# Layer norms between the stages of a two-block model: order of shifts and copies, splits per pair of tiles, place of the sums, and the queue of two small loads

## The chip, the cores and the metric

The kernel runs on one core of a Trainium2 chip, in one launch. The metric is the time of the execution on the device in microseconds (us), lower is better. A run gives one time; the median of several is compared. The profile is of one further execution.

## What is computed

Two transformer-like blocks over x of 512 tokens by 1024 channels, all in float32. The part that matters here is what stands between the matrix products: after each residual addition there is a norm over the 1024 channels of a token, and its result is the input of the next product.

```python
def first_block(...):
    h = x + mixer(rmsnorm(x, g_mix))              # conv, pooling, then y @ w_out   ("out")
    h = h + swiglu(rmsnorm(h, g_ffn), ...)        # norm 1; gate/up "gu0", "down0"
    return rmsnorm(h, g_final)                    # norm 2

def second_block(x, ...):                         # alpha = DN_ALPHA = sqrt(2)
    h = fox_attention(x)                          # "qkv1", "out1"
    x = layer_norm(alpha * x + h, g, b)           # norm 3
    x = layer_norm(alpha * x + conv_ffn(x), g, b) # "gu1", "down1", norm 4
    k1, k2, v = shared_kv(x)                      # rotary tables cos, sin
    h = diff_attention(x, k1, k2, v)              # "qkv2", "out2"; uses lambda
    x = layer_norm(alpha * x + h, g, b)           # norm 5
    x = layer_norm(alpha * x + conv_ffn(x), g, b) # "gu2", "down2", norm 6
    return x

def layer_norm(x, g, b):
    mu = mean(x); var = mean((x - mu) ** 2)
    return (x - mu) * rsqrt(var + 1e-5) * g + b
```

## The kernel before

Channels lie on the 128 partitions, in DT = 8 tiles of 128; tokens are the free axis, S = 512 wide. The residual is `xres` (128 x 8 x 512). For precision every product is done as three: an operand X is split into a high part XH (rounded to the fast matmul format) and a low part XL = X - XH, and likewise each weight tile into WH and WL; `product` (L875 to L877) multiplies XL with WH, XH with WH and XH with WL.

**Weights** come in items of up to 128 x 8 x 128. SyncE loads an item into one of two buffers `raw` (L482; it waits for `w_lo`, the split of the item two before). ScalarE writes WH in two instructions (`high`, L1371), GpSimd writes WL in two (`low`, L675), into one of four slots; TensorE then uses the item. A slot comes free with `item_done`.

**A norm in halves.** The six norms m = 1 to 6 at the ends of the stages out, down0, out1, down1, out2 and down2 are done for two halves h of 256 tokens, so that the first half can be normed while TensorE still works on the second half of the last items. Norms 1 and 2 are RMS norms; norms 3 to 6 are centred (mean and shift). The order of work is written out by hand on each engine:

- TensorE, end of the old stage (`stage`, `down`): the first half of the last two items (`half_item` or `part` with h = 0), the second half of the item before the last (24 products of 128x256), `half_stats(m, 0)` (one-column products that sum x and x squared over the channels, L1044 and L1046; 24 of them in norms 3 and 5), the first 6 of 8 steps of the last item's second half, `half_widen(m, 0)` (root and mean are spread over the partitions, L1033), the last 2 steps. Then the new stage begins in `stage_in_halves`: for each half and tile k four products with XH (L971, L972; wait for `x_top`) and, one tile behind, two with XL (L959; wait for `x_lo`). `half_stats(m, 1)` stands at tile 2 and `half_widen(m, 1)` at tile 4 of the first half.
- VectorE (`norm_in_halves`, L1845 to L1869): adds the tail tiles, computes the moments from the sums, and norms tiles in pairs. For norms 3 to 6 a pair is one multiplication by the root (L1865, both tiles, 128x512, one operand in PSUM) and one multiply-and-add for each tile (L1869, 128x256, its inputs `xres` and the shift buffer in SBUF). For norms 1 and 2 it is one instruction for each tile (L1861), with an operand in PSUM. Each signals `xn_ready`. The order is pair 0, second half's tail, pairs 1 and 2, the moments of the second half, pair 3, then the four pairs of the second half.
- ScalarE (`norm_in_halves`, L1397 to L1421): squares of the tail (L1397), the root (L1381), and `pair(h, p)`: `shifts` (L1408, one 128x256 instruction for each tile, into one of three pair buffers, free again when VectorE has used it), then a copy of each tile into XH (L1421, 128x256, signals `x_top`). The next pair's shifts stand behind the copies of this one. Between the halves it does `high` of the new stage's third item.
- GpSimd (`lows_of_halves`): for each tile XL = x - XH (L708, 128x256, signals `x_lo`), with `low` of the third item between the halves.

**Two small loads** are issued by ScalarE in the middle of a norm, through the argument `tail_done`: `load_gates` in norm 2 (2 DMAs) and `load_rope` in norm 4 (6 DMAs: the rotary tables, 128x512 in one and four of 32x512, and the lambda parameters). Both first wait for the last item of the old stage, since their buffers overlap with those of the stage. VectorE waits for the rope tables after norm 4; ScalarE waits for the gates after norm 2. SyncE at that time has issued the first four weight items of the new stage; its fifth (loop index n = 4) waits for the split of the third.

## Time and profile before

| what | value |
|---|---|
| median of 3 runs | 1907.21 us (1903.19 to 1908.96) |
| profiled execution | 1903.91 us, of which the span from first to last instruction 1902.1 us |
| TensorE busy | 1829.4 us (96%) |
| GpSimd busy | 1036.0 us (54%) |
| ScalarE busy | 781.4 us (41%) |
| VectorE busy | 768.8 us (40%) |
| mean granted TensorE clock | 0.979 |

Engines are written PE (TensorE), DVE (VectorE), ACT (ScalarE), POOL (GpSimd) and SP (SyncE); a q behind a name marks the engine's queue of DMA issues. A row of the timeline gives the start in us from the begin of the span, the time that the instruction (or the group "xN" of equal neighbours) took, the line of the kernel, output and inputs, their shape, and in brackets the idle time before it with what ended it. "issue" means that the profile shows nothing that was waited for.

### The profile page before, as it was taken

The numbers are of one execution on the slowest core, as the hardware profiler recorded it, in microseconds if no ns is written. First come the engines' busy times: TensorE is split into PE (matmuls) and PEld (weight loads), VectorE is DVE, ScalarE is ACT, GpSimd is POOL, SyncE is SP. The second block draws the span as 40 slices with busy tenths as digits, with TensorE's granted clock in tenths as the row PEclk, the third lists the DMA queues.
The fourth block names the chain that finished last, engine by engine and source line by source line (L and its number), as shares of the span: only waits on it lengthen the run. The fifth ranks groups of instructions, "written<-read, shape, count | busy, mean of one in ns | idle before, by whom it ended". The sixth has DMA issues, their size and how long they took to land.

```text
span 1902.1 us, 27192 instructions
## 1 busy us (share of the span) xinstructions
PE 1829.4 (96%) x8895; PEld 1522.8 (80%) x8895; DVE 768.8 (40%) x1389; ACT 781.4 (41%) x1638; POOL 1036.0 (54%) x937
## 2 busy tenths in 40 slices
PE   6999999999999999899999999889998999999997
PEld 5878888888887888788888888878886888888887
DVE  6964000001135455564333322456655743333224
ACT  4433332322244455345444422445554454444223
POOL 5866655655462322356666654555554566666551
PEclk7999999999999999999999999899999999999998
DMA  4303333323333444223333233233232233332331
GB/s 123 100 18 94 100 92 103 91 84 105 90 99 95 118 112 115 75 76 93 95 99 99 77 106 93 68 78 84 69 80 67 73 94 97 90 99 86 99 91 67
DMA packets 328499, 170.88 MB, mean 90 GB/s; under 512 B 43426, under 2 KB 318964, under 8 KB 328436
## 3 DMA queue, kind: packets, MB, share of 16 engines
q1 hardware_dynamic: 327026, 169.49, 32.1%
q10 hardware_dynamic: 1410, 0.59, 0.1%
q8 instruction: 35, 0.57, 0.1%
q14 instruction: 28, 0.23, 0.0%
HBM read 151.10 MB, written 2.10 MB: 81 GB/s over the span
## 4 chain that ended last, share of the span: by engine, by line
PE 79%; ACT 4%; DVE 4%; SPq 3%; issue 3%; DMA 3%; POOL 3%; ACTq 0%; DVEq 0%; POOLq 0%
PE bank L875 23%; PE bank L877 22%; PE bank L876 22%; PE attended L875 2%; PE attended L876 2%; PE attended L877 2%; SPq L639 2%; DMA raw<-in_kv_w 1%; DVE xres L1869 1%; DVE small L2027 1%; POOL XL L708 1%; ACT pmap L1582 1%; POOL WL L675 1%; ACT XH L1421 1%; PE turned L1212 1%
## 5 line engine op out<-in xcount | busy, mean ns | idle before, releaser
L675 POOL TENSOR_TENSOR WL<-raw,WH 128x512 fp32r<-128x512 f32 (+3 forms) x656 | 786.0, 1221 | 618.5 <-ACT WH L1371 617.7
L875 PE MATMUL bank<-XL,WH 128*128 128x512 f32 x1456 | 580.5, 399 | 10.0 <-ACT work L1597 5.2
L877 PE MATMUL bank<-XH,WL 128*128 128x512 f32 x1456 | 568.8, 391 | 0.0
L876 PE MATMUL bank<-XH,WH 128*128 128x512 f32 x1456 | 567.7, 390 | 0.0
L1371 ACT ACTIVATE WH<-raw 128x512 fp32r<-128x512 f32 (+3 forms) x656 | 338.4, 566 | 352.1 <-PE bank L877 197.1
L875 PEld LDWEIGHTS bank<-XL,WH 128*128 128x128 f32 x1456 | 275.0, 189 | 65.5 <-issue 8.1
L877 PEld LDWEIGHTS bank<-XH,WL 128*128 128x128 f32 x1456 | 274.7, 189 | 58.1
L876 PEld LDWEIGHTS bank<-XH,WH 128*128 128x128 f32 x1456 | 275.4, 189 | 51.6
L877 PE MATMUL bank<-HH,WL 128*128 128x512 f32 (+1 forms) x528 | 201.1, 381 | 0.0
L876 PE MATMUL bank<-HH,WH 128*128 128x512 f32 (+1 forms) x528 | 201.1, 381 | 0.0
L875 PE MATMUL bank<-HL,WH 128*128 128x512 f32 (+1 forms) x528 | 201.0, 381 | 0.0
L1978 DVE SCALAR_TENSOR_TENSOR xres<-xres,bank 128x512 f32 (+1 forms) x39 | 26.7, 686 | 267.2 <-PE bank L877 266.8
L790 POOL TENSOR_TENSOR HL<-hid,HH 128x512 f32 x66 | 85.1, 1289 | 70.5 <-ACT HH L1537 70.5
L876 PEld LDWEIGHTS bank<-HH,WH 128*128 128x128 f32 x528 | 99.1, 188 | 21.2
L877 PEld LDWEIGHTS bank<-HH,WL 128*128 128x128 f32 x528 | 99.1, 188 | 21.2
L875 PEld LDWEIGHTS bank<-HL,WH 128*128 128x128 f32 x528 | 99.1, 188 | 21.1
L1582 ACT ACTIVATE pmap<-score,small 128x128 f32<-128x128 f32 (+3 forms) x128 | 67.1, 525 | 90.6 <-DVE small L2027 90.5
L2001 DVE TENSOR_TENSOR hid<-bank,act_g 128x512 f32<-128x512 f32 x21 | 14.5, 692 | 207.4 <-PE bank L877 203.9
L2027 DVE TENSOR_REDUCE small<-score 128x1 f32<-128x128 f32 (+3 forms) x128 | 62.4, 488 | 80.7 <-PE score L1197 52.0
L2084 DVE SCALAR_TENSOR_TENSOR hid<-bank,par,hid 128x511 f32<-128x511 f32 x42 | 31.5, 750 | 150.7 <-ACT hid L1660 150.5
L1660 ACT ACTIVATE hid<-bank,par 128x512 f32<-128x512 f32 x42 | 32.7, 779 | 143.5 <-PE bank L877 143.5
L2084 DVE SCALAR_TENSOR_TENSOR act_g<-bank,par,act_g 128x511 f32<-128x511 f32 x42 | 31.5, 750 | 128.2 <-ACT act_g L1660 128.2
(278 smaller groups left out, 2579.3 us busy)
## 6 DMA issues: line engine op xcount, KB each, us to landing
raw<-in_ffn_w_in SPq DMA_DIRECT2D x88, 512.0 KB, 3.8
raw<-in_w_gate SPq DMA_DIRECT2D x22, 512.0 KB, 3.8
raw<-in_w_up SPq DMA_DIRECT2D x22, 512.0 KB, 3.9
raw<-in_ffn_w_out SPq DMA_DIRECT2D x28, 384.0 KB, 3.4
raw<-in_ffn_w_out SPq DMA_DIRECT2D x28, 320.0 KB, 3.1
raw<-in_a_w_in SPq DMA_DIRECT2D x16, 512.0 KB, 4.1
raw<-in_kv_w SPq DMA_DIRECT2D x32, 256.0 KB, 3.8
raw<-in_w_in SPq DMA_DIRECT2D x12, 512.0 KB, 3.9
```

What stands on the lines that cost most here:

```text
L639: sp.dma_start(z[r, c, :].bitcast(F32), x[r, slot, 0, :].bitcast(F32)).then_inc(q_padded, 16)
L675: pool.tensor_tensor(wl, x, wh, ALU.subtract).then_inc(w_lo, 1)
L790: pool.tensor_tensor(HL[:, bass.ds(it * 2 + j, 1), :], hid[:, j:j + 1, :], HH[:, bass.ds(it * 2 + j, 1), :].bitcast(F32), ALU.subtract).th ...
L875: pe.matmul(out_, wh, xl, start=start, stop=False)
L876: pe.matmul(out_, wh, xh, start=False, stop=False)
L877: return pe.matmul(out_, wl, xh, start=False, stop=stop)
L1371: act.activation(wh, x, ACT.Copy).then_inc(w_hi, 1)
L1582: act.activation(pmap[:, n % 4, 0:k], sc[c][:, 0:k], ACT.Exp, bias=small[:, n % 4:n % 4 + 1], accum_out=small[:, 4 + n % 4:5 + n % 4]).the ...
L1660: act.activation(dst[:, j, :], ff_banks(it, j)[side][:, :], ACT.Identity, bias=ff_par(layer - 1, 3, n), scale=ff_par(layer - 1, 2, n)).the ...
L1978: dve.scalar_tensor_tensor(out=r, in0=r, scalar=factor, in1=bank[j][:, :].rearrange("p (a s) -> p a s", a=1), op0=ALU.mult, op1=ALU.add).t ...
L2027: dve.tensor_reduce(small[:, n % 4:n % 4 + 1], sc[c][:, 0:(n // 2 + 1) * P], AX_X, ALU.max, negate=True).then_inc(mx[c], 1)
L2084: own.link(dve.scalar_tensor_tensor(out=dst[:, j, 1:], in0=src[:, 0:S - 1], scalar=ff_par(layer - 1, 1, n), in1=dst[:, j, 1:], op0=ALU.mul ...
```

## The change

Five edits:

1. On ScalarE `pair` is taken apart into `shifted_pair` (shifts) and `tops` (copies). The shifts of pair p+1 stand ahead of the copies of pair p; in the second half `copies(0)` (output copies, norm 6 only) moves behind the shifts of pair 2.
2. Copies into XH and the splits XL = x - XH are done for two tiles by one instruction (128x512), except for tiles 0 and 1 of each half (`TILES_OF_HALF`).
3. On TensorE `half_stats(m, 0)` stands behind the first 4 of 8 steps of the half item, instead of behind all 8, in `stage` and in `down`.
4. `load_gates` is issued by SyncE at n = 4 of the qkv1 loop, ahead of the weight load of that index.
5. `load_rope` is issued by SyncE at n = 4 of the qkv2 loop, likewise.

```diff
+TILES_OF_HALF = ((0, 1), (1, 1), (2, 2), (4, 2), (6, 2))
...
+            def load_gates():
+                sp.wait_ge(item_done, STAGES["qkv1"][0])
+                sp.dma_start(wf[:, :, :], a_in[:, :, 3 * D:3 * D + FOX_HEADS]).then_inc(wf_in, 16)
+                sp.dma_start(small[0:FOX_HEADS, 48:49], A["a_b_f_2"].rearrange("o h -> h o")).then_inc(wf_in, 16)
...
             for n in range(4 * UNITS + 8):
                 u, j = divmod(n - 4, 4)
+                if n == 4:
+                    load_gates()
...
+            def load_rope():
+                sp.wait_ge(item_done, STAGES["qkv2"][0])
+                sp.dma_start(rope[:, 0, :], A["rope"][0]).then_inc(rope_in, 16)
+                for b in range(4):
+                    r = 0 if b >= 2 else 32
+                    sp.dma_start(rope[32 * b:32 * b + 32, 1, :], A["rope"][1][r:r + 32, :]).then_inc(rope_in, 16)
+                sp.dma_start(lamr[:, :], A["b_lambda_2"].rearrange("o a d -> o (a d)")).then_inc(rope_in, 16)
...
                 u, j = divmod(n - 5, 4)
+                if n == 4:
+                    load_rope()
...
-                    for t in range(DT):
-                        i = DT * h + t
-                        pool.wait_ge(x_top, half_tile(m, h, t) + 1)
-                        src = pairs_of[i // 2 % 3][:, i % 2, :] if m == 1 else xres[:, t, c]
-                        pool.tensor_tensor(XL[:, t, c], src, XH[:, t, c].bitcast(F32), ALU.subtract).then_inc(x_lo, 1)
+                    for t, n in TILES_OF_HALF:
+                        src = pairs_of[(DT * h + t) // 2 % 3][:, t % 2:t % 2 + n, :] if m == 1 else xres[:, t:t + n, c]
+                        pool.wait_ge(x_top, half_tile(m, h, t) + n)
+                        pool.tensor_tensor(XL[:, t:t + n, c], src, XH[:, t:t + n, c].bitcast(F32), ALU.subtract).then_inc(x_lo, n)
...
-                half_item(name, DT - 2, 0, hi, lo, 0, DT, 1).then_inc(item_done, 1)
+                half_item(name, DT - 2, 0, hi, lo, 0, DT, 1, 0, 4)
                 half_stats(m, 0)
+                half_item(name, DT - 2, 0, hi, lo, 0, DT, 1, 4).then_inc(item_done, 1)
...
-                part(2, 1).then_inc(item_done, 1)
+                part(2, 1, 0, 4)
                 half_stats(m, 0)
+                part(2, 1, 4).then_inc(item_done, 1)
...
-                def pair(h, p):
+                def tops(h, p):
+                    if not follower:
+                        return
                     c = slice(h * HALF, (h + 1) * HALF)
+                    for t, w in TILES_OF_HALF:
+                        if t // 2 != p:
+                            continue
+                        act.wait_ge(xn_ready, DT + half_tile(m, h, t) + w)
+                        src = pairs_of[(DT * h + t) // 2 % 3][:, t % 2:t % 2 + w, :] if m == 1 else xres[:, t:t + w, c]
+                        act.activation(XH[:, t:t + w, c], src, ACT.Copy).then_inc(x_top, w)
+
+                def shifted_pair(h, p):
                     if n in CENTRED:
                         shifts(h, p)
-                    if not follower:
-                        return
-                    for t in (2 * p, 2 * p + 1):
-                        i = DT * h + t
-                        act.wait_ge(xn_ready, DT + half_tile(m, h, t) + 1)
-                        src = pairs_of[i // 2 % 3][:, i % 2, :] if m == 1 else xres[:, t, c]
-                        act.activation(XH[:, t, c], src, ACT.Copy).then_inc(x_top, 1)
 
                 squares_of(0)
                 root(n, 0)
-                pair(0, 0)
+                shifted_pair(0, 0)
+                shifted_pair(0, 1)
+                tops(0, 0)
                 squares_of(1)
                 tail_done()
-                pair(0, 1)
-                pair(0, 2)
+                shifted_pair(0, 2)
+                tops(0, 1)
+                shifted_pair(0, 3)
+                tops(0, 2)
                 root(n, 1)
-                pair(0, 3)
+                tops(0, 3)
                 if follower:
                     high(Nth(STAGES[follower][0] + 2), UNIT[2] if follower[0] == "q" else DT)
-                for p in range(DT // 2):
-                    pair(1, p)
-                    if p == 1:
-                        copies(0)
+                shifted_pair(1, 0)
+                shifted_pair(1, 1)
+                tops(1, 0)
+                shifted_pair(1, 2)
+                copies(0)
+                tops(1, 1)
+                shifted_pair(1, 3)
+                tops(1, 2)
+                tops(1, 3)
                 copies(1)
...
-            norm_in_halves(2, "qkv1", tail_done=load_gates)
+            norm_in_halves(2, "qkv1")
...
-            norm_in_halves(4, "qkv2", "ffn", load_rope)
+            norm_in_halves(4, "qkv2", "ffn")
```

## Rows read from the trace of the kernel before

**Rows 1.** The page, part 1: busy us, share and instructions of each engine.
```profile
PE 1829.4 (96%) x8895; PEld 1522.8 (80%) x8895; DVE 768.8 (40%) x1389; ACT 781.4 (41%) x1638; POOL 1036.0 (54%) x937
```

**Rows 2.** Windows, norm 3: stretch, busy us of PE, PEld, DVE, ACT, POOL, clock.
```profile
835.80:858.90 23.10, 17.93 (x126) 16.69 (x126) 16.55 (x33) 16.70 (x39) 14.26 (x18) 0.93 0.08 24
```

**Rows 3.** Timeline of TensorE in norm 3; columns as told above.
```profile
836.80 0.38 PE L971 MATMUL bank<-XH,WH 128*128 128x256 f32 x1 [1.00 <-ACT XH L1421]
...
839.40 0.39 PE L971 MATMUL bank<-XH,WH 128*128 128x256 f32 x1 [1.15 <-ACT XH L1421]
...
840.22 0.28 PE L1044 MATMUL turned<-ones,work 128*128 128x1 f32 x2
...
842.82 0.36 PE L971 MATMUL bank<-XH,WH 128*128 128x256 f32 x1
...
858.81 0.40 PE L875 MATMUL attended<-XL,WH 128*128 128x512 f32 x1
```

**Rows 4.** Timeline of ScalarE in norm 3, second half: copies, shifts, copies.
```profile
854.24 0.81 ACT L1421 ACTIVATE XH<-xres 128x256 fp32r<-128x256 f32 x2 [0.51 <-DVE xres L1869]
854.96 1.00 ACT L1408 ACTIVATE work<-turned,par 128x256 f32<-128x256 f32 x2
856.49 0.82 ACT L1421 ACTIVATE XH<-xres 128x256 fp32r<-128x256 f32 x2 [0.52 <-DVE xres L1869]
```

**Rows 5.** Timelines of VectorE and GpSimd in norm 3, single instructions.
```profile
848.91 1.49 DVE L1869 SCALAR_TENSOR_TENSOR xres<-xres,par,work 128x256 f32<-128x256 f32 x1
848.66 1.47 POOL L675 TENSOR_TENSOR WL<-raw,WH 128x512 fp32r<-128x512 f32 x1
...
853.37 0.83 DVE L1869 SCALAR_TENSOR_TENSOR xres<-xres,par,work 128x256 f32<-128x256 f32 x1 [0.41 <-ACT work L1408]
853.19 0.74 POOL L708 TENSOR_TENSOR XL<-xres,XH 128x256 fp32r<-128x256 f32 x1
```

**Rows 6.** Single lines over the span: duration ns min/median/max, shapes.
```profile
L790 POOL TENSOR_TENSOR HL<-hid,HH x66: 1276/1289/1301, 193.9 to 1761.2; 128x512 f32 x66
L1371 ACT ACTIVATE WH<-raw x656: 293/617/636, 12.4 to 1865.0; 128x512 fp32r<-128x512 f32 x109, 128x384 fp32r<-128x384 f32 x36, 128x256 fp32r<-128x256 f32 x19
```

**Rows 7.** Timelines in norm 4: ScalarE with its queue, TensorE, SyncE's queue.
```profile
1214.50 0.36 ACTq L1680 DMA_DIRECT2D rope<-in_rope  x1
...
1217.37 1.02 ACT L1408 ACTIVATE work<-score,par 128x256 f32<-128x256 f32 x2 [2.48 <-issue]
...
1219.03 0.58 PE L971 MATMUL bank<-XH,WH 128*128 128x256 f32 x1 [3.43 <-ACT XH L1421]
...
1229.96 0.37 SPq L616 DMA_DIRECT2D raw<-in_b_w_q  x1
```

**Rows 8.** Windows: the stretches at half clock, and the one ahead of norm 4's.
```profile
844.20:847.60 3.40, 3.40 (x19) 3.40 (x17) 2.24 (x5) 2.96 (x7) 1.58 (x3) 0.50 0.00 0
...
1212.90:1216.30 3.40, 1.70 (x13) 1.29 (x11) 1.86 (x5) 1.81 (x5) 1.44 (x2) 1.00 0.13 35
1216.30:1229.90 13.60, 10.87 (x51) 10.87 (x52) 7.31 (x17) 7.42 (x18) 5.79 (x8) 0.50 0.10 31
```

**Rows 9.** Timelines in norm 1 (GpSimd, TensorE) and norm 2 (TensorE).
```profile
184.16 5.61 POOL L708 TENSOR_TENSOR XL<-work,XH 128x256 fp32r<-128x256 f32 x8
...
190.16 0.40 PE L875 MATMUL attended<-XL,WH 128*128 128x512 f32 x1
...
545.70 0.39 PE L971 MATMUL bank<-XH,WH 128*128 128x256 f32 x1 [0.46 <-ACT XH L1421]
```

**Rows 10.** Timeline of VectorE in norm 6.
```profile
1884.54 0.88 DVE L1869 SCALAR_TENSOR_TENSOR xres<-xres,par,work 128x256 f32<-128x256 f32 x2 [0.47 <-ACT work L1408]
...
1893.69 0.90 DVE L1869 SCALAR_TENSOR_TENSOR xres<-xres,par,work 128x256 f32<-128x256 f32 x2 [0.32 <-ACT work L1408]
```

**Rows 11.** Timelines in norm 2: ScalarE's square of the tail, TensorE's first sum.
```profile
537.29 0.40 ACT L1397 ACTIVATE work<-xres 128x256 f32<-128x256 f32 x1
...
539.26 0.28 PE L1044 MATMUL score<-ones,work 128*128 128x1 f32 x2
```

More of the change, by code:

```diff
@@ L1557, in _ @@
             warm(ACT.Sqrt)
-            def load_gates():
-                act.wait_ge(item_done, STAGES["qkv1"][0])
-                act.dma_start(wf[:, :, :], a_in[:, :, 3 * D:3 * D + FOX_HEADS]).then_inc(wf_in, 16)
-                act.dma_start(small[0:FOX_HEADS, 48:49], A["a_b_f_2"].rearrange("o h -> h o")).then_inc(wf_in, 16)
-            norm_in_halves(2, "qkv1", tail_done=load_gates)
+            norm_in_halves(2, "qkv1")
             act.wait_ge(wf_in, 32)
@@ L1676, in _ @@
             warm(ACT.Sqrt)
-            def load_rope():
-                act.wait_ge(item_done, STAGES["qkv2"][0])
-                act.dma_start(rope[:, 0, :], A["rope"][0]).then_inc(rope_in, 16)
-                for b in range(4):
-                    r = 0 if b >= 2 else 32
-                    act.dma_start(rope[32 * b:32 * b + 32, 1, :], A["rope"][1][r:r + 32, :]).then_inc(rope_in, 16)
-                act.dma_start(lamr[:, :], A["b_lambda_2"].rearrange("o a d -> o (a d)")).then_inc(rope_in, 16)
-            norm_in_halves(4, "qkv2", "ffn", load_rope)
+            norm_in_halves(4, "qkv2", "ffn")
             def sub_root(u):
```

## The prediction

> **What bounds the kernel now.** I read the page first: TensorE is busy for 96% of the span [rows 1]. So only time in which TensorE stands still, or runs at half clock, can be won or lost, and the change touches it in six places: the layer norms at the ends of the stages "out", "down0", "out1", "down1", "out2" and "down2" (norms 1 to 6 below). A norm is short: norm 3 takes 23.1 us from the last product of one stage to the first full item of the next, and TensorE is busy for 17.9 us of it [rows 2]. The timelines of the engines inside one norm are the view that counts. In norm 3 TensorE waits before its first tile (1.00 us) and its third (1.15 us), each time for ScalarE's copy into XH, and starts its next item at 858.81 [rows 3]. In the second half of the norm the copies of one pair of tiles come 2.25 us after those of the pair before (854.24, 856.49), although TensorE has only twelve products of 0.12 us per pair, 1.44 us: here the ring ScalarE shift, VectorE, ScalarE copy sets the pace [rows 4].
>
> **One cost that the change meets.** VectorE's second step of a pair (L1869, two operands in SBUF) takes 0.48 us alone, two of them 0.88 [rows 10], but 0.83 at 853.37 and 1.49 at 848.91 [rows 5]. Both times a subtraction of GpSimd was running. The subtraction from 848.66 took 1.47 us, to 850.13, and L1869 ended at 850.40; the one from 853.19 ended at 853.93, and L1869 at 854.20. Each time L1869 ends 0.28 us after GpSimd. GpSimd pays too: 1.47 us instead of its usual 1.29 [rows 5, 6]. So the two take turns, one whole instruction at a time, and a longer GpSimd instruction is a longer turn.
>
> Beside this the Trainium skill, "SBUF — State Buffer", section "SBUF: two separate sides", says that a VectorE operation with two SBUF inputs and a GpSimd operation that reads SBUF lock each other out: whichever starts first has the port pair for its whole instruction. It speaks against splits per pair. The trace agrees that the loser waits, but L1869 at 853.37 needs only 0.28 us behind GpSimd, not its whole 0.48. Taken literally the rule would make a pair 0.33 us longer than my sum below has it, over two pairs in each of three norms 2 us in all.
>
> **Part 1, order and pair splits, norm 3.** What moves, step by step:
> - Two more shifts stand ahead of the first copy. Two shifts occupy ScalarE for 0.9 to 1.0 us [rows 4], of which it waited 0.3 to 0.4 for VectorE anyway; the first copy, and with it TensorE's first tile (836.80 [rows 3]), comes 0.6 us later.
> - Tiles 2 and 3 are copied by one instruction, which needs VectorE's result for tile 3 (0.4 us later) and takes 0.62 us, as a 128x512 copy does, instead of 0.42 [rows 6]. TensorE's third tile, now at 839.40 [rows 3], comes at 840.1: +0.7. The second half's sums stand behind it on TensorE, then the moments, the root and the widening: the second half starts 0.7 us late.
> - Tiles 6 and 7 of the first half: +0.4 and +0.2 again ahead of the split. One split of 128x512 takes 1.25 to 1.29 us (L790 has this shape) [rows 6] against 1.40 to 1.44 for two of 128x256 (eight take 5.61 [rows 9]): -0.15. So GpSimd starts the two weight splits of 1.29 us 1.15 us later, and the first pair of the second half, whose L1869s queue behind these [rows 5], ends 1.15 us later, at 851.55 instead of 850.40.
> - Pairs 2 and 3 of that half. Let L1869 of a pair end at T. The joint copy ends at T+0.66, and GpSimd asks at T+0.74. VectorE has meanwhile done L1865 (0.68) and runs the next first L1869 from T+0.63 to T+1.11. GpSimd goes next, 1.14 us behind it (the rest of the 1.47 after 848.98), to T+2.27, and the second L1869 ends at T+2.55. That is 2.55 against 2.25: +0.3 for each of two pairs. With splits of 128x256 and the new order the pace would be about 1.8.
> - The last pair: from L1869's end to the end of the last split 0.62 + 0.12 + 1.29 = 2.03. Now the first tile's copy starts 0.4 us before that point: 0.42 + 0.12 + 1.44 - 0.40 = 1.58. So +0.45; and TensorE then has four low products left instead of two, +0.24.
> Sum: 1.15 + 0.3 + 0.3 + 0.45 + 0.24 = 2.44. Laid out the same way, the order of before comes to 858.75, where the trace has 858.81 [rows 3]. I take +2.4 for norm 3 and as much for norm 5, which has the same rows 670 us later. Both are followed by a stage that TensorE bounds, so it all arrives at the end.
>
> **Norms 1 and 2** have no shifts, and their VectorE step reads PSUM, so nothing takes turns. GpSimd bounds the end: eight splits in 5.61 us from 184.16 [rows 9]; as two singles and three pairs they take 2 x 0.70 + 3 x 1.25 = 5.15, -0.45. Against this the sums come 0.5 us later (tile 2 waits for tile 3), and the split of tiles 6 and 7 another 0.6 (second tile and longer copy), less 0.15: GpSimd ends 0.55 late. TensorE gets tiles 2 and 3 together at 187.8 and has 28 products of 0.118 us left after them, to 191.3 instead of 190.16 [rows 9]: +1.1. In norm 2 the same would be lost, but the two gate loads no longer hold ScalarE (TensorE's 0.46 us wait at 545.70 [rows 9]) and the weight split there is half as long: +0.3.
>
> **Part 2, loads on the weight queue.** In norm 4 ScalarE issues six loads after the first pair; its next work starts 2.48 us late at 1217.37, and TensorE waits 3.43 us at 1219.03, against 1.15 in norm 3 [rows 3, 7]. The change gives ScalarE back 2.85 us (1214.50 to 1217.37). On SyncE the loads wait for the stage's last item, as they did on ScalarE. What is queued behind that wait is the weight load of qkv2's fifth item, which is issued only at 1229.96 [rows 7], since it waits for a split inside the norm. Six issues end by about 1216.5: 13 us of cover, cost nothing. If that cover were gone each issue would cost 0.4 to 0.5. The gate loads lie in front of the same kind of wait. Norm 4 also pays part 1's +2.5: together -0.3.
>
> **Part 3, sums amid the half item.** They start 12 products (1.4 us) earlier. The widening behind them keeps its place in TensorE's order, and did not wait before, so the gain is 0. The cost is cover: in norm 2 the tail's square ends at 537.69, behind a table load, and the sums go from 539.26 to 537.84 [rows 11]; 0.15 us is left. Bounds: 0 to +0.3 over six norms. I take 0.
>
> **Norm 6** has no splits, only the new order. VectorE's waits of 0.47 us (1884.54) and 0.32 us (1893.69) for a shift [rows 10] go: -0.75.
>
> **Clock.** Norm 3 has 3.4 us at the lower of the two levels (1.2 instead of 2.4 GHz), behind the 24 one-column products; norm 4 has 13.6 us at it, behind a stretch with 1.70 of 3.40 us busy [rows 8]. In norm 4 that costs about 2 us. The new norms 3, 4 and 5 wait 1.9 and then 1.4 us early in the first half, more than norm 3 does now and less than norm 4. So the clock may fall there: norm 4 then wins nothing back, and the sums in norms 3 and 5, 2.6 us from 840.22 to 842.82 [rows 3], take 5.2. Bounds: -2 (norm 4 regains all, no other falls) to +5 (both fall). I take 0, nearer to norm 3, the row with the milder waits.
>
> **How the numbers follow.** 1.1 + 0.3 + 2.4 + 2.4 - 0.3 - 0.75 + 0 + 0 = +5.2 us. The profiled execution took 1903.91 us (span 1902.1 us), so its counterpart should show 1909.1; the median of the runs shown, 1907.21, gives 1912.4. A measurement of this kernel can tell about 0.3%, 5.7 us, from no change.
> - Forecast, 0.43: +5.2, between +2 and +8. It straddles the bound, 0.24 within and 0.19 slower.
> - Rival A, slower, 0.26: the clock. Its place is the first half of norms 3 and 5, its price 2.6 us each when the sums run at the lower level, and it decides when the early waits of 1.9 and 1.4 us drop the clock before the sums. 5.2 + 5.2 = +10.4: 1917.6. For it: norm 4 now. Against it: norm 3 now survives waits of 1.00 and 1.15.
> - Rival B, 0.20: pair splits do not lengthen the turns (VectorE gets both its steps in ahead of GpSimd). Then a pair takes some 1.8 us instead of 2.55 and norms 3 and 5 cost nothing; 1.1 + 0.3 - 2.8 - 0.75 = -2.2: 1905.0. Against it: at 848.91 GpSimd, which had asked first, came between two L1869s.
> - Rival C, faster, 0.11: rival B, and the clock stays up in norm 4 and behind it; -2.2 - 2 - 2 = -6.2: 1901.0.
> Slower by over 0.3%: 0.19 + 0.26 = 0.45. Faster: 0.11. Within: 0.24 + 0.20 = 0.44. The range reaches from 1904 to 1919: it leaves out C and the far end of A.
>
> **What would show it.** In the changed profile: first copy of norm 3 about 0.6 us later after the widening; L1869 next to a 128x512 split at 1.3 to 1.5 us; copies of neighbouring pairs about 2.55 us apart; TensorE's start of the next item 2.4 us later in norms 3 and 5; no issue gap in norm 4 and the six loads on SP's queue; norm 6 0.75 us shorter; the sums early without a wait. The prediction is wrong if L1869 stays near 0.5 us beside pair splits, if the half-clock stretches differ by more than one in TensorE-bound time, or if the sums wait for the squares.

## The result, and the profile after

| | before | after |
|---|---|---|
| median of 5 runs each | 1906.56 us (1903.19 to 1908.96) | 1917.26 us (1913.09 to 1918.89) |
| profiled execution (span) | 1903.91 us (1902.1) | 1913.09 us (1910.3) |
| mean granted TensorE clock | 0.979 | 0.977 |

The changed kernel is slower: ratio 1.0054, 95% interval 1.0034 to 1.0073. The predicted time was 1912.4 us, in a range from 1904 to 1919; the forecast's own +5.2 us (between +2 and +8) came out as +10.7, nearly the figure of rival A (1917.6). The profiled execution of the changed kernel is the fastest of its five; the other four took 1916.93 to 1918.89 us, with a mean granted clock of 0.972 to 0.975.

The page's part 1, after (to set beside [rows 1]): the work is the same, ScalarE and GpSimd have 30 instructions less each, and VectorE is busy 9.4 us longer with as many instructions as before.

```profile
PE 1837.7 (96%) x8895; PEld 1530.5 (80%) x8895; DVE 778.2 (41%) x1389; ACT 775.7 (41%) x1608; POOL 1033.1 (54%) x907
```

The length of each norm says where the time went. I measure it from the first widening on TensorE to the first full item of the next stage (norm 6: to TensorE's last instruction), in the one profiled execution of each kernel:

| norm | before | after | difference | predicted |
|---|---|---|---|---|
| 1 | 16.72 | 18.12 | +1.40 | +1.1 |
| 2 | 15.75 | 16.26 | +0.51 | +0.3 |
| 3 | 24.31 | 27.04 | +2.73 | +2.4 |
| 4 | 26.81 | 27.08 | +0.27 | -0.3 |
| 5 | 24.30 | 30.23 | +5.93 | +2.4 |
| 6 | 18.04 | 17.29 | -0.75 | -0.75 |

That is +10.1 us. Ahead of norm 1 and between the norms the two executions differ by -1.9 us; three stretches carry it, -1.53 ahead of norm 1, -1.71 between norms 2 and 3, +1.30 between norms 4 and 5, and the change touches nothing there. The span grew by 8.2.

Windows of norms 3, 4 and 5, before and then after (stretch, length, busy us of PE, PEld, DVE, ACT, POOL, granted clock, DMA share, GB/s); the last two lines lie inside norm 5:

```profile
834.50:858.81 24.31, 19.14 (x137) 17.70 (x135) 17.23 (x34) 17.35 (x39) 14.26 (x18) 0.93 0.08 23
1211.85:1238.66 26.81, 21.17 (x128) 20.12 (x127) 15.37 (x31) 16.73 (x38) 13.55 (x19) 0.75 0.16 40
1503.61:1527.91 24.30, 19.17 (x136) 17.72 (x135) 17.24 (x34) 17.33 (x39) 14.25 (x18) 0.93 0.08 23
```
```profile
833.19:860.23 27.04, 20.52 (x137) 19.11 (x136) 20.47 (x34) 15.97 (x33) 13.86 (x12) 0.87 0.07 21
1213.27:1240.35 27.08, 21.65 (x129) 19.73 (x128) 18.70 (x31) 15.54 (x33) 13.63 (x13) 0.81 0.16 39
1506.60:1536.83 30.23, 24.22 (x137) 23.17 (x136) 20.51 (x34) 15.97 (x33) 13.85 (x12) 0.72 0.06 18
1511.60:1521.90 10.30, 9.67 (x45) 9.67 (x46) 4.82 (x12) 2.40 (x6) 2.67 (x2) 0.50 0.01 2
1528.70:1535.50 6.80, 5.94 (x28) 5.94 (x29) 6.05 (x9) 3.71 (x6) 3.56 (x3) 0.50 0.18 55
```

In all three norms VectorE's 34 or 31 instructions take 3.2 to 3.3 us longer than before. And norms 3 and 5, equal in instructions, are no longer equal in time: norm 5 spends 17 us at the lower level of TensorE's clock (granted 0.50), 10.3 of them in its first half, where norm 3 has two stretches of 3.4 us. TensorE reaches the first tile of the second half 19.3 us after the widening in norm 5 and 16.3 us after it in norm 3, so the difference arises in the first half.

**The turns.** Timelines of norm 5 after, second half: ScalarE's copies, then VectorE and GpSimd:

```profile
1528.88 0.63 ACT L1439 ACTIVATE XH<-xres 128x512 fp32r<-128x512 f32 x1 [0.69 <-DVE xres L1888]
...
1531.42 0.63 ACT L1439 ACTIVATE XH<-xres 128x512 fp32r<-128x512 f32 x1 [1.00 <-DVE xres L1888]
1533.95 0.63 ACT L1439 ACTIVATE XH<-xres 128x512 fp32r<-128x512 f32 x1 [1.90 <-DVE xres L1888]
```
```profile
1532.36 1.50 DVE L1888 SCALAR_TENSOR_TENSOR xres<-xres,par,work 128x256 f32<-128x256 f32 x1
1532.19 1.38 POOL L725 TENSOR_TENSOR XL<-xres,XH 128x512 fp32r<-128x512 f32 x1 [1.15 <-ACT XH L1439]
```

The pairs come 2.54 and 2.53 us apart, where [rows 4] has 2.25. L1888 (L1869 of before) takes 1.50 us beside a split of 128x512: GpSimd ends at 1533.57, VectorE at 1533.86, 0.29 us behind it, as the 0.28 in [rows 5].

**The queue.** SyncE's queue in norm 4 after; the six loads are out by 1217.14, and the weight load behind them is issued at 1230.63:

```profile
1214.61 0.34 SPq L651 DMA_DIRECT2D rope<-in_rope  x1
1214.99 1.82 SPq L654 DMA_DIRECT2D rope<-in_rope  x4
1216.86 0.28 SPq L655 DMA_DIRECT2D lamr<-in_b_lambda  x1
1230.63 0.40 SPq L624 DMA_DIRECT2D raw<-in_b_w_q  x1
```

**TensorE early in the half.** In norm 5 after, two waits for ScalarE's copies, which norms 3 and 4 have with the same lengths (1.62 and 1.25 us in both), where [rows 3] has 1.00 and 1.15 and [rows 7] 3.43:

```profile
1509.53 0.39 PE L989 MATMUL bank<-XH,WH 128*128 128x256 f32 x1 [1.62 <-ACT XH L1439]
...
1512.23 0.58 PE L989 MATMUL bank<-XH,WH 128*128 128x256 f32 x1 [1.24 <-ACT XH L1439]
```

### The profile page after: what moved, and what is told of

Read it like the earlier page. It is cut to its first block and busy times, and to the rows that moved or that the text cites. A ratio compares the mean times of both kernels' runs of the same rounds, so it can differ in the third digit from the quotient of the medians.

```text
span 1910.3 us, 27192 instructions
## 1 busy us (share of the span) xinstructions
PE 1837.7 (96%) x8895; PEld 1530.5 (80%) x8895; DVE 778.2 (41%) x1389; ACT 775.7 (41%) x1608; POOL 1033.1 (54%) x907
```

## The experiments

Theory T: in norms 3 to 5 the pair splits lengthen the turns that VectorE and GpSimd take, and the pair of tiles is a coarser grain everywhere; the lower clock comes on top. Its rivals: the order or the place of the sums costs the time, or the clock alone does. All ratios are to runs of the kernel before beside them (medians 1905.1 to 1906.0 us), with 95% intervals.

| kernel | median us | ratio |
|---|---|---|
| after, all single tiles | 1903.05 | 0.9978 (0.9964 to 0.9992) |
| after, GpSimd's splits single | 1910.80 | 1.0026 (1.0015 to 1.0037) |
| before + loads on SyncE | 1899.88 | 0.9966 (0.9953 to 0.9979) |
| before + early sums | 1907.88 | 1.0010 (1.0001 to 1.0019) |
| before + pairs | 1919.16 | 1.0073 (1.0059 to 1.0086) |
| before + order | 1902.81 | 0.9983 (0.9971 to 0.9995) |
| after + filler products | 1913.73 | 1.0046 (1.0032 to 1.0059) |
| after, second operand in PSUM | 1897.10 | 0.9963 (0.9945 to 0.9981) |
| before, second operand in PSUM | 1899.69 | 0.9970 (0.9960 to 0.9979) |
| weight split moved ahead | 1889.32 | 0.9921 (0.9907 to 0.9935) |
| the same + filler products | 1888.99 | 0.9917 (0.9902 to 0.9931) |

### The pairs taken back out of the change

All single tiles:

```diff
-TILES_OF_HALF = ((0, 1), (1, 1), (2, 2), (4, 2), (6, 2))
+TILES_OF_HALF = tuple((t, 1) for t in range(8))
```

> The changed kernel with every copy and every split back to one tile (order, queue and place of the sums stay changed). Theory T (turns): the pair splits are what costs, since each holds VectorE's L1888 (L1869 before) for a whole 128x512 instruction. Then norms 3 and 5 (widening to the next full item) go from 27.0 and 30.2 us to about 24 us, copies of neighbouring pairs come less than 2.2 us apart, L1888 never takes 1.5 us except beside the weight splits, and the kernel is at or below the time before (ratio 0.997 to 1.001). Theory O (order): two shifts ahead of the first copy are the cost; then norm 3 stays above 25.5 us and the ratio near 1.003 to 1.005.

And only GpSimd's splits single (the loop of `lows_of_halves`), with ScalarE's copies still in pairs:

```diff
-                    for t, n in TILES_OF_HALF:
+                    for t, n in [(t, 1) for t in range(DT)]:
```

> The changed kernel with GpSimd's splits of x back to one tile each, ScalarE's copies still in pairs. Theory T: the length of the GpSimd instruction is what matters; norm 3 comes to about 25.6 us (1.1 below the changed kernel by the steps of the prediction), the rest above 24.3 being the wait of the joint copy for its second tile; ratio about 1.001 to 1.003. Rival G (grain): the joint copy and the arrival of two tiles at once are the cost and GpSimd's instruction length is not; then it stays at the changed kernel's time, 1.004 to 1.006.

With all tiles single the change is faster than before, 0.9978; norms 1 to 6 take 16.72, 15.03, 23.99, 21.94, 23.98 and 17.28 us. So the pairs cost 1.0054 - 0.9978, about 0.76% or 14 us, and the rest of the change gains. (The profiled execution took 1893.56 us and is the fastest of twelve, which reach up to 1905.42: its norm lengths are those of an execution with little half clock, and norm 4 above all can't be compared by them.)

GpSimd's share in it is the smaller one. Timeline of ScalarE in norm 3, with single splits and paired copies:

```profile
856.18 0.63 ACT L1439 ACTIVATE XH<-xres 128x512 fp32r<-128x512 f32 x1 [0.69 <-DVE xres L1888]
858.17 0.63 ACT L1439 ACTIVATE XH<-xres 128x512 fp32r<-128x512 f32 x1 [0.45 <-DVE xres L1888]
860.16 0.63 ACT L1439 ACTIVATE XH<-xres 128x512 fp32r<-128x512 f32 x1 [1.36 <-DVE xres L1888]
```

The pace falls from 2.54 to 1.99 us, and norm 3 from 27.04 to 26.17 (25.6 was expected), both with the clock at 0.87: single splits give back about 0.9 us there, and 0.1 us or less in norms 1 and 2. Over the kernel it is 0.28%, or some 5 us, more than 0.9 us in each of three norms; norm 5 (28.99 us against 30.23) and norm 4 also differ in their clock, and that part was not taken apart. The other 0.48% hangs on the paired copies. Norm 1 shows it where nothing takes turns: 18.03 with paired copies alone, 18.12 after, 16.72 with single tiles.

### The parts of the change, each alone on the kernel before

The loads on SyncE:

```diff
+                if n == 4:
+                    load_rope()
...
-            norm_in_halves(4, "qkv2", "ffn", load_rope)
+            norm_in_halves(4, "qkv2", "ffn")
```

(and `load_gates` likewise)

> The kernel before with only the two small loads moved to SyncE's queue. Prediction: norm 4 (widening to next full item) falls from 26.8 to about 22 to 24 us, since the issue gap of 2.5 us goes and with it most of the half-clock stretch; nothing else moves; ratio 0.997 to 0.999. Rival: the loads come later or hold SyncE's weight load, then norm 4 or the start of qkv2 waits for a DMA and the ratio is 1.000 or more.

The sums amid the half item:

```diff
-                half_item(name, DT - 2, 0, hi, lo, 0, DT, 1).then_inc(item_done, 1)
+                half_item(name, DT - 2, 0, hi, lo, 0, DT, 1, 0, 4)
                 half_stats(m, 0)
+                half_item(name, DT - 2, 0, hi, lo, 0, DT, 1, 4).then_inc(item_done, 1)
```

(and in `down` likewise)

> The kernel before with only the sums of the first half moved amid the half item. Prediction: no norm changes its length, ratio 0.9995 to 1.0005. Rival: TensorE now waits for the square of the tail (up to 0.3 us in each down stage), or the one-column products next to the wait ahead of the first tile pull the clock down (1.7 us each time): ratio 1.001 to 1.003.

Copies and splits of pairs in the old order (`shifted_pair(h, p)` and `tops(h, p)` right behind each other):

```diff
+TILES_OF_HALF = ((0, 1), (1, 1), (2, 2), (4, 2), (6, 2))
...
+                def pair(h, p):
+                    shifted_pair(h, p)
+                    tops(h, p)
```

> The kernel before with pair copies and pair splits alone (old order of shifts, loads on ScalarE, sums in their old place). Theory T (turns and grain of the pairs): norms 1 and 2 take 18.1 and about 17 us (16.7 and 15.8 before), norm 3 and 5 about 27.1 (24.3), the pace of the copies in the second half 2.5 us or more; ratio 1.004 to 1.007, as much as the whole change costs or more, since the gain of the queue is missing. Rival (the parts only hurt together): ratio below 1.003.

The new order with single tiles:

```diff
+TILES_OF_HALF = tuple((t, 1) for t in range(8))
...
-                pair(0, 0)
+                shifted_pair(0, 0)
+                shifted_pair(0, 1)
+                tops(0, 0)
```

(and so on, as in the change)

> The kernel before with the new order of shifts and copies alone, one tile per instruction. By the steps of the prediction norms 3 and 5 take 23.9 us instead of 24.3, norms 1 and 2 stay, norm 6 is 0.75 us shorter; norm 4 keeps its issue gap and about 26.5 us. Ratio 0.998 to 1.000. Rival: the later first copy costs more than the ring gains, or drops the clock; norm 3 above 25 us and ratio above 1.001.

The queue alone is worth 0.34%, and norm 4 takes 24.20 us, just above what was expected (22 to 24). But norm 5, in which nothing was changed and whose early waits are as before, takes 26.05 us (clock 0.80) instead of 24.30 (0.93) in this profile. TensorE in norm 4 with it, in place of the 3.43 us of [rows 7]:

```profile
1212.41 0.38 PE L988 MATMUL bank<-XH,WH 128*128 128x256 f32 x1 [1.00 <-ACT XH L1438]
...
1214.69 0.58 PE L988 MATMUL bank<-XH,WH 128*128 128x256 f32 x1 [0.82 <-ACT XH L1438]
```

The sums alone move no norm by more than 0.04 us in the profile; 1.0010 (1.0001 to 1.0019) lies above the expected range, but is hardly apart from no change, and no profile shows where its 0.1% would lie. The order alone gains 0.17%, although it brings a first wait of 1.62 us. Norm 5 takes 23.96 us, as expected (23.9), norm 3 25.17 us at a clock of 0.86, norm 4 26.07 and norm 6 16.48:

```profile
837.61 0.38 PE L972 MATMUL bank<-XH,WH 128*128 128x256 f32 x1 [1.62 <-ACT XH L1421]
...
839.74 0.38 PE L972 MATMUL bank<-XH,WH 128*128 128x256 f32 x1 [0.69 <-ACT XH L1421]
```

The pairs alone cost 0.73%. ScalarE in norm 3 with them, old order: the copies come 2.82 and 2.84 us apart. Norms 1 to 5 take 18.16, 16.68, 29.8, 30.5 and 29.45 us; norms 3 and 5 are 2.7 and 2.4 us above what was expected (27.1), with the clock at 0.83 and 0.81. VectorE's second step beside a split of two tiles takes at most 1.16 us in this order, not 1.5, and yet the pace is slower than the changed kernel's 2.54: the turns are not the whole cost of the pairs.

```profile
856.50 0.63 ACT L1420 ACTIVATE XH<-xres 128x512 fp32r<-128x512 f32 x1 [0.70 <-DVE xres L1876]
859.32 0.63 ACT L1420 ACTIVATE XH<-xres 128x512 fp32r<-128x512 f32 x1 [1.29 <-DVE xres L1876]
862.16 0.63 ACT L1420 ACTIVATE XH<-xres 128x512 fp32r<-128x512 f32 x1 [1.29 <-DVE xres L1876]
```

The four parts add up to -0.34 + 0.10 + 0.73 - 0.17 = +0.32%, against 0.54% for the whole. The five intervals together leave about 0.3% open, so this is no sign of a part that works only in company.

### The turn itself taken away

VectorE's second step reads a PSUM bank instead of the shift buffer in SBUF, in the kernel after and in the kernel before. Both versions leave the shift out of the result of norms 3 to 6, so they don't compute the layer norm; they only measure what the place of the operand does to the time:

```diff
-  scalar=pcol(f"ln_{gain}_g_2", t + (DT if m > 4 else 0)), in1=dst[:, j, :],
+  scalar=pcol(f"ln_{gain}_g_2", t + (DT if m > 4 else 0)), in1=wide_rstd[h][:, 0:HALF],
```

> The changed kernel with the second operand of L1888 taken from the bank of the widened root in PSUM instead of the shift buffer in SBUF: the shift is left out of norms 3 to 6, the number and the shape of all instructions stay. Theory T (turns between a VectorE instruction with two SBUF operands and a GpSimd instruction): L1888 takes 0.5 us everywhere, pair splits beside it or not; the copies of neighbouring pairs come 1.6 to 1.7 us apart instead of 2.54; norms 3 and 5 (full clock) take about 22.4 us instead of 26.7. Rival G (grain alone): L1888's 1.5 us have another cause and norms 3 and 5 stay above 25.5 us.

> The kernel before with the same edit (shift left out of norms 3 to 6). Theory T: norms 3 and 5 fall from 24.3 to about 22.1 us, so before and changed kernel come within 0.5 us of each other in these norms once the turns are gone; what the changed kernel keeps is the loss in norms 1 and 2 and the gain of the queue in norm 4. Rival: the gap of 2.5 us per norm between the two orders stays.

L1888 by source line, first in the kernel after and then with the PSUM operand (count, then duration in ns as min/median/max, first and last start); the operand's bank is called `score` in the first half and `turned` in the second:

```profile
L1888 DVE SCALAR_TENSOR_TENSOR xres<-xres,par,work x64: 472/485/1517, 834.5 to 1903.8; 128x256 f32<-128x256 f32 x64
```
```profile
L1888 DVE SCALAR_TENSOR_TENSOR xres<-xres,par,score x32: 473/478/482, 835.2 to 1883.7; 128x256 f32<-128x256 f32 x32
L1888 DVE SCALAR_TENSOR_TENSOR xres<-xres,par,turned x32: 472/478/481, 848.0 to 1889.7; 128x256 f32<-128x256 f32 x32
```

The same instruction never takes over 0.482 us, beside whatever split. ScalarE's copies in norm 3, with the PSUM operand, after and then before:

```profile
850.64 0.65 ACT L1439 ACTIVATE XH<-xres 128x512 fp32r<-128x512 f32 x1
852.05 0.66 ACT L1439 ACTIVATE XH<-xres 128x512 fp32r<-128x512 f32 x1
853.46 0.63 ACT L1439 ACTIVATE XH<-xres 128x512 fp32r<-128x512 f32 x1 [0.75 <-DVE xres L1888]
```
```profile
851.39 0.81 ACT L1421 ACTIVATE XH<-xres 128x256 fp32r<-128x256 f32 x2 [0.16 <-DVE xres L1869]
853.27 0.81 ACT L1421 ACTIVATE XH<-xres 128x256 fp32r<-128x256 f32 x2 [0.16 <-DVE xres L1869]
```

The pace is 1.41 us a pair in the changed kernel and 1.88 in the one before: without turns the change has the quicker pace, with turns the slower one (2.54 against 2.25). The windows of norm 3 (after) and of norm 5 (before), chosen because both have the clock at 0.92:

```profile
833.91:856.46 22.55, 18.61 (x137) 17.59 (x135) 14.45 (x34) 15.29 (x33) 12.95 (x12) 0.92 0.08 25
```
```profile
1500.02:1521.91 21.89, 18.91 (x136) 17.67 (x135) 14.45 (x34) 17.29 (x39) 13.85 (x18) 0.92 0.09 25
```

VectorE is busy for 14.45 us in both, and the gap is 0.66 us instead of 2.7 (within 0.5 was expected). The other two norms of the kind can't be compared so, since their clocks differ: norm 5 of the changed kernel takes 25.56 us at 0.80, norm 3 of the kernel before 23.4 at 0.85.

Over the kernel the two stand at 1897.10 against 1899.69 us, with overlapping intervals: of the 10.7 us by which the change was slower nothing is left. The changed kernel still has the gain of the queue in it, 6.5 us by the run with the loads alone. Without turns the rest of the change thus costs about 4 us (6.5 - 2.6), of which norms 1 and 2 make 1.9, and with turns about 17 (10.7 + 6.5); both are estimates, uncertain by some 5 us. That shows that the turns make the larger part of the loss. It doesn't divide them into the length of GpSimd's splits and the joint copy's wait for its second tile; for that the runs with single tiles stand, 0.28 and 0.48%.

### The clock

After, with products that nobody reads put where TensorE waits in the first half of norms 3 to 5 (twelve ahead of tile 0, eight ahead of tile 2):

```diff
+                def filler(k):
+                    for _ in range({0: 12, 2: 8}.get(k, 0)):
+                        pe.matmul(tb[1][:, HALF:], WH[:, g % SLOTS, 0, :], WH[:, (g + 1) % SLOTS, 0:2, :], start=True, stop=True)
...
+                        if h == 0 and NORM[m] in CENTRED:
+                            if k == 0:
+                                pe.wait_ge(w_lo, 2 * (g + 2))
+                            filler(k)
```

> The changed kernel with 12 products of 128x256 ahead of the first tile and 8 ahead of the third in norms 3, 4 and 5, written to a part of a bank that nobody reads: they lie in TensorE's waits of 1.6 and 1.2 us and change nothing else. Theory K (clock): part of the loss is that these waits drop the granted clock before or in the sums. Then the stretches at half clock in norms 3 to 5 get fewer or shorter, norm 5 falls from 30.2 to about 27 us, norm 4 from 27.1 to about 25, and the ratio falls from 1.0054 to about 1.002 to 1.003. If the one-column products alone decide the clock, the half-clock stretches stay as they are and the ratio stays at 1.004 to 1.006.

And the changed kernel as it is, a second time:

> The changed kernel once more, for a second profile of it. If the half-clock stretches depend on how the execution falls on the clock's own time, norm 5 (30.2 us in the first profile) and norm 3 (27.0) change places or lengths by 1.5 to 3.5 us between the profiles, while the order and the lengths of the instructions on VectorE, ScalarE and GpSimd stay. If not, the lengths repeat within 0.3 us.

Windows of norms 3, 4 and 5 in that second execution (1919.0 us):

```profile
837.31:867.66 30.35, 24.34 (x136) 23.32 (x135) 20.53 (x34) 15.95 (x33) 13.87 (x12) 0.72 0.06 18
1220.70:1246.41 25.71, 20.29 (x128) 18.51 (x127) 18.97 (x31) 15.53 (x33) 13.59 (x13) 0.87 0.16 41
1513.59:1543.76 30.17, 24.13 (x136) 23.00 (x135) 20.52 (x34) 15.95 (x33) 13.87 (x12) 0.72 0.06 18
```

VectorE, ScalarE and GpSimd are busy for the same times as in the first execution, to 0.3 us. Yet norm 3, 27.04 us there, takes 30.35 here, with the granted clock at 0.72 instead of 0.87. So which norms fall to the lower level differs between executions of one kernel, and one norm more or less costs 3.1 to 3.3 us (30.17, 30.23 and 30.35 against 27.04). The two profiled executions, with one and two long norms, took 1913.09 and 1919.0 us; the median of the first five runs, 1917.26, is nearer to the second. The long norms are not all of that difference, though: the six norms together differ by 1.9 us (norm 3 +3.3, norm 4 -1.4), and the stretches ahead of and between them, which hold the same instructions, by 5.0 us.

With filler, norm 5 takes 27.06 us at 0.87, norm 3 27.62 at 0.88 and norm 4 25.76 at 0.93, and the median falls by 3.5 us to 1913.73. Norm 5 is as Theory K had it, but the ratio, 1.0046, lies in the range of its rival, and the intervals, 1.0032 to 1.0059 and 1.0034 to 1.0073, overlap.

The profiles of all versions say more together. A stretch of about 10 us at the lower level in norm 3 or 5 is found in 4 of 6 norms whose early waits are 1.62 and 1.25 us (the changed kernel twice, GpSimd's splits single). It is in 1 of 2 with 1.62 and 0.90 (after, operand in PSUM), in 1 of 2 with 1.00 and 1.8 (before + pairs) and in 1 of 2 of the version with the weight split moved ahead, below (0.53 and 1.15 in the norm that has it). It is in none of 8 with 1.00 and 1.15 (before, + loads, + early sums, operand in PSUM), in none of 4 with 1.62 and 0.69 (all single tiles, before + order), and in none of 4 with filler. That speaks for the early waits as a cause of the lower clock. Since norms with equal waits come out either way, the waits alone don't decide it.

### A version that beats both

The kernel before, with the loads on SyncE and single tiles. The split of the third weight item (`high` on ScalarE, `low` on GpSimd), which stood between the halves, goes ahead of the norm's root and first tile, where both engines have idle time. The new order stays in the second half and in norm 6 only, so that TensorE's first tiles come no later:

```diff
+                low(Nth(STAGES[follower][0] + 2), UNIT[2] if follower[0] == "q" else DT)
...
-                    if h == 0:
-                        low(Nth(STAGES[follower][0] + 2), UNIT[2] if follower[0] == "q" else DT)
...
+                if follower:
+                    high(Nth(STAGES[follower][0] + 2), UNIT[2] if follower[0] == "q" else DT)
```

> A version built on what the runs show: the kernel before with the two loads on SyncE's queue, one tile per instruction, the new order of shifts only in the second half of the norm (and in all of norm 6), and the split of the new stage's third weight item moved ahead of the root, where ScalarE and GpSimd wait anyway. Theory T: the weight split no longer stands in front of the L1869s and the last splits; norms 3 and 5 take about 21.5 us (24.3 before), norm 4 about 20.5 to 22 (26.8), norm 1 about 14.6 (16.7), norm 2 about 13.9 (15.8), norm 6 17.3. Together about 14 us less: ratio 0.991 to 0.994. If the weight split hid in something else all along, norms 1 to 5 keep their length and the ratio is that of the queue and the order alone, 0.996.

The same with seven filler products ahead of tile 0 and seven ahead of tile 2:

> The early-split version (e8) with 7 products of 128x256 ahead of the first and 7 ahead of the third tile in norms 3 to 5, 0.8 us each, inside TensorE's waits of 1.0 and 1.15 us; they write where nobody reads. Theory K (the early waits drop the clock): norms 3 and 5 fall from 25.5 and 23.5 to 21.5 to 23 us, ratio 0.989 to 0.991. If the one-column sums alone decide, nothing moves: 0.991 to 0.994.

GpSimd in norm 3 of the first: the weight split is over before the first tile arrives.

```profile
825.35 2.50 POOL L693 TENSOR_TENSOR WL<-raw,WH 128x512 fp32r<-128x512 f32 x2 [4.51 <-ACT WH L1387]
832.61 1.44 POOL L727 TENSOR_TENSOR XL<-xres,XH 128x256 fp32r<-128x256 f32 x2 [4.77 <-ACT XH L1436]
```

0.9921 and 0.9917: 15.8 and 16.8 us less than the kernel before took beside them. Norm 4 takes 20.69 us in both, at clock 1.00. Norms 3 and 5 take 25.51 and 23.52 us without filler, where 21.5 was expected, and 21.64 and 21.65 with it; norms 1 and 2 take 14.87 and 14.20 (14.6 and 13.9 expected):

```profile
829.82:855.33 25.51, 23.11 (x136) 21.92 (x135) 16.83 (x34) 16.01 (x37) 12.11 (x16) 0.76 0.06 17
```
```profile
829.65:851.29 21.64, 20.54 (x150) 19.38 (x149) 16.99 (x34) 15.79 (x36) 12.10 (x16) 0.92 0.09 25
```

By the profiles the filler gains 5.7 us in these two norms; the medians are 1889.32 and 1888.99, and the ratio with filler, 0.9917, lies where Theory K's rival had it. Since a norm's clock differs between executions, two profiles can't carry that comparison, and this pair gives the filler no effect that can be measured.

## Why the prediction was right, and where it was not

- **The number.** The forecast's own +5.2 us, between +2 and +8, was missed: the medians differ by 10.7, close to rival A's +10.4. That the time still lies within 1904 to 1919 is owed to rival A, whose reason is only half borne out (below), and so in part to luck.
- **What bounds the change** was read rightly: the change's loss lies in the six norms (+10.1 us of profiled time), and the long stages between them hand on what the norms lose, but for the 1.9 us by which the rest of the two executions differs. VectorE's and GpSimd's work per norm, not their share of the span, decided.
- **The turns** held in number: 2.55 us a pair was worked out (its own terms, 1.11 + 1.14 + 0.28, give 2.53) and 2.54 and 2.53 are in the trace; L1888 beside a pair's split was put at 1.3 to 1.5 us and takes up to 1.52. The Trainium skill, "SBUF — State Buffer", section "SBUF: two separate sides", says of a VectorE operation with two SBUF inputs and a GpSimd operation that reads SBUF that whichever starts first gets the shared port pair for its whole instruction, while the other fully blocks. The trace agrees that one waits for the other, and with the operand in PSUM, one SBUF input instead of two, the wait is gone (0.473 to 0.482 us in all 64). If the loser then ran its whole 0.48 us, as the prediction read the rule literally, the pace would be 2.88 (an estimate); but it ends 0.29 us behind the winner. Rival B, which had no longer turns, falls: its pace was 1.8.
- **Norms 1 and 2**: +1.40 and +0.51 against +1.1 and +0.3. The step was right (the grain of the copies, in GpSimd-bound norms), each term 0.2 to 0.3 us short: in norm 1 GpSimd starts the splits of the second half 1.23 us later after the widening than before, where the steps give 0.95. The 28 products of 0.118 us are 3.3 us and not the 3.5 that the prediction added; the trace has 3.45 for that stretch.
- **Norm 3**: +2.73 against +2.4, and the steps came out one by one: TensorE's first tile 0.62 us later after the widening (0.6 foreseen), its third 0.73 (0.7), the end of the second half's first pair 1.30 (1.15), that of the last split 2.48 (2.2), TensorE behind it 0.25 (0.24). Norm 3 has 3.4 us more at the lower clock than before, but in its second half, where TensorE afterwards still waits 0.50 us for the last copy:

```profile
858.21 0.39 PE L989 MATMUL bank<-XH,WH 128*128 128x256 f32 x1 [0.50 <-ACT XH L1439]
```

- **Norm 6**: -0.75, as worked out. That it fits so exactly is luck: norm 6 also ends in stretches at the lower clock, and with the same instructions in it as after the change the run with the order alone shows 16.48 us instead of 17.29, and with those of before the run with the loads alone 17.18 instead of 18.04. The step itself is in the trace. VectorE's waits for shifts there, by the view of waits, fell from 1.0 us to 0.2:

```profile
DVE xres L1869 <- ACT work L1408: 1.0, 3, 0.5
```
```profile
DVE xres L1888 <- ACT work L1427: 0.2, 1, 0.2
```

- **The queue**: the cover was put at 13 us and is 13.5 (1217.14 to 1230.63). ScalarE's 2.85 us came back: with the loads alone moved, norm 4 takes 24.20 us instead of 26.81. In the whole change norm 4 came to +0.27 instead of -0.3 in the first profile and to -1.10 in the second: part 1 took the gain back, as the sum has it, and the clock moves the rest.
- **Sums**: worth 0 by the sum; no norm changed when they alone were moved.
- **The term that was mis-sized is the clock.** The prediction had norm 4 as the one place where the early waits drop it, took 0 and gave rival A a chance of 0.26. Its sum has nothing for it, and the runs showed 3.1 to 3.3 us for each of norms 3 and 5 that falls to the lower level in its first half. In the first profiled execution norm 5 does, for 10.3 us there and 17 in all, and takes 3.5 us more than the +2.4 of the sum; in the second norms 3 and 5 both do, at 30.35 and 30.17 us. Two such norms are 6.4 us, and the forecast missed the median by 5.5; but the runs behind the median have no profile, and two executions differ by up to 5 us outside the norms as well, so that the miss is theirs is likely and not shown. Rival A had the place and nearly the price (2.6 a norm foreseen for the sums alone; more than the sums runs at the lower level). Its reason is only half borne out. The waits came as predicted in kind (1.9 and 1.4 foreseen, 1.62 and 1.24 found). But norm 3 of the first execution has the same 1.62 and 1.25 and stays up until behind the sums. The prediction's ground against A, that norm 3 survived waits of 1.00 and 1.15, was one execution's word on something that differs from one execution to the next. One of the prediction's own signs of being wrong thus came true in part: norms 3 to 5 have five stretches at the lower level instead of three, 34 us instead of 20.5, and the longest of those in norm 5 lies where TensorE bounds the norm.
- What stays open: whether the waits ahead of the sums or the one-column sums themselves bring the clock down, and what decides it in a given execution. The filler products gained 3.5 us once, within the intervals, and nothing the second time. The count over all profiles speaks for the waits, but these are one or two executions of each version. Nor was the place of the second half's sums, behind the third tile, varied in any run.

## What to carry to other kernels

Before joining instructions to save their fixed cost, look whom their length holds up: here 0.15 us saved per GpSimd split lengthened each turn that VectorE waits for, and a pair of tiles delayed the consumer of the first. If two engines take turns, try first to move one operand to PSUM (measured here only in kernels that leave the shift out) or the long instructions to where the other engine is idle (with the loads moved and part of the new order, 0.8% here) before rearranging the order. A term for the clock should be costed as a chance per place over several executions, since one profile shows only one draw.

## What the runs showed of the hardware

- The same instructions in the same order run with norm 3 at 27.04 us (clock 0.87) in one execution and at 30.35 us (0.72) in another. I had taken stretches at the lower level for a property of the kernel.
- The lower level also comes where waits are short: with the loads alone moved, norm 4 has waits of 1.00 and 0.82 us and still a mean clock of 0.79, and norm 5 of the same run, with waits of 0.99 and 1.14 us, one of 0.80:

```profile
1210.11:1234.31 24.20, 20.84 (x129) 19.81 (x127) 15.34 (x31) 16.60 (x38) 13.54 (x19) 0.79 0.18 44
```

- The waiting VectorE instruction needs only some 0.28 us behind GpSimd's end, of the 0.48 it takes alone, and with one operand in PSUM it is not held up at all (473 to 482 ns in 64 of 64).
